# State mixing of a two-layer hybrid block: chunks of 128 tokens, two heads at a time, against chunks of 64 tokens, all heads at once

## What is computed

```python
def step(S, inp):
    r_t, w_t, k_t, v_t, kk_t, a_t = inp
    sa = jnp.einsum('bhvk,bhk->bhv', S, -kk_t)
    S = (S * w_t[:, :, None, :] + sa[..., None] * (kk_t * a_t)[:, :, None, :]
         + v_t[..., None] * k_t[:, :, None, :])
    return S, jnp.einsum('bhvk,bhk->bhv', S, r_t)
S0 = jnp.zeros((bsz, A_HEADS, A_HEAD_DIM, A_HEAD_DIM), f32)   # 8 heads of 64 x 64
_, o = lax.scan(step, S0, xs)
```

## Time and profile before

| | |
|---|---|
| median of 3 executions | 1030.74 us (1028.5 to 1035.65) |
| span of the profiled execution | 1026.6 us |
| what lies around the span, median less span | 4.1 us |
| PE busy | 1008.1 us |
| DVE busy | 816.6 us |
| ACT busy | 616.9 us |
| DMA, mean | 160 GB/s |

### The profile page before, as it was taken

How to read it: one execution, slowest core, us unless ns; L and a number is a source line. 1 busy time by engine, 2 the same in 40 slices (tenths; PEclk the granted TensorE clock), 3 DMA queues, 4 the chain that set the end, 5 groups by cost and what they waited for, 6 DMA issues and landing times.

```text
span 1026.6 us, 22212 instructions
## 1 busy us (share of the span) xinstructions
PE 1008.1 (98%) x8278; PEld 932.0 (91%) x8278; DVE 816.6 (80%) x1365; ACT 616.9 (60%) x967; POOL 11.9 (1%) x30
## 2 busy tenths in 40 slices
PE   8999999999999999999999999999999999999997
PEld 7998988899999999999999989789999999998886
DVE  6799763897797898878778996649977878888785
ACT  7964333656556665666689533246656565667665
POOL 0000000100000000000000000010000000000000
PEclk9999999999999999999999999999999999999999
DMA  8452342335545565555544534224445545565554
GB/s 301 148 182 103 104 146 81 114 111 178 162 154 179 180 209 183 189 185 184 191 142 145 185 99 144 88 74 142 139 153 167 182 164 185 172 219 185 192 192 152
DMA packets 46392, 164.42 MB, mean 160 GB/s; under 512 B 5888, under 2 KB 6064, under 8 KB 46304
## 3 DMA queue, kind: packets, MB, share of 16 engines
q1 hardware_dynamic: 44640, 160.19, 46.8%
q0 software_dynamic: 800, 1.33, 0.6%
q10 hardware_dynamic: 864, 1.63, 0.5%
HBM read 161.56 MB, written 1.05 MB: 158 GB/s over the span
## 4 chain that ended last, share of the span: by engine, by line
PE 86%; DVE 9%; ACT 2%; issue 2%; DMA 1%; SPq 0%; DVEq 0%; ACTq 0%
PE psum L471 85%; DVE sb_lo L1317 2%; ACT sb_rw L927 1%; DVE sb_inv L1566 1%; DVE sb_inv L1525 1%; DMA sb_x<-x_t 1%; DVE sb_inv L1528 1%; PE psum L789 1%; ACT sb_hh L927 0%; DVE sb_rw L1609 0%; DVE sb_yf L1590 0%; DVE sb_qb L1375 0%; ACT sb_hi L927 0%; DVE sb_rw L1496 0%; DVE sb_inv L1502 0%
## 5 line engine op out<-in xcount | busy, mean ns | idle before, releaser
L927 ACT ACTIVATE sb_hi<-sb_raw 128x1024 fp32r<-128x1024 f32 (+1 forms) x298 | 310.4, 1052 | 170.7 <-PE psum L471 161.2
L1317 DVE TENSOR_TENSOR sb_lo<-sb_raw,sb_hi 128x1024 fp32r<-128x1024 f32 x296 | 358.0, 1219 | 53.2 <-ACT sb_hi L927 52.9
L471 PE MATMUL psum<-sb_hh,sb_hi 128*128 128x256 f32 x1184 | 344.2, 291 | 3.2 <-DVE sb_hl L1324 2.1
L471 PE MATMUL psum<-sb_hl,sb_hi 128*128 128x256 f32 x1184 | 335.3, 283 | 0.0
L471 PE MATMUL psum<-sb_hh,sb_lo 128*128 128x256 f32 x1184 | 335.1, 283 | 0.0
L471 PE MATMUL psum<-sb_o,sb_hi 128*128 128x256 f32 (+1 forms) x1376 | 276.0, 314 | 1.3 <-DVE sb_o L1338 1.3
L471 PEld LDWEIGHTS psum<-sb_hh,sb_hi 128*128 128x128 f32 x1184 | 227.0, 192 | 17.9 <-issue 10.9
L471 PEld LDWEIGHTS psum<-sb_o,sb_hi 128*128 128x128 f32 x1376 | 224.1, 191 | 14.6 <-DVE sb_o L1338 1.7
L471 PEld LDWEIGHTS psum<-sb_hl,sb_hi 128*128 128x128 f32 x1184 | 227.3, 192 | 0.8 <-issue 0.5
L471 PEld LDWEIGHTS psum<-sb_hh,sb_lo 128*128 128x128 f32 x1184 | 227.2, 192 | 0.0
L471 PE MATMUL psum<-sb_o,sb_lo 128*128 128x256 f32 x880 | 193.9, 283 | 0.0
(11 more groups left out here) (187 smaller groups left out, 1027.7 us busy)
## 6 DMA issues: line engine op xcount, KB each, us to landing
sb_raw<-w_stream SPq DMA_DIRECT2D x299, 512.0 KB, 3.3
sb_pm<-mix_par ACTq DMA_DIRECT2D x2, 512.5 KB, 3.4
y_t<-sb_rw SPq DMA_DIRECT2D x4, 256.0 KB, 2.1
sb_cf<-const_f SPq DMA_DIRECT2D x1, 550.0 KB, 9.3
sb_pm<-mix_par SPq DMA_DIRECT2D x1, 512.5 KB, 10.9
sb_raw<-w_stream SPq DMA_DIRECT2D x2, 256.0 KB, 4.4
sb_x<-x_t ACTq DMA_DIRECT2D x2, 256.0 KB, 4.4
sb_x<-x_t SPq DMA_DIRECT2D x1, 512.0 KB, 6.7
```

Source lines behind the costliest of these rows:

```text
L471: return pe.matmul(out, lhsT, rhs, start=start, stop=stop, skip_group_check=True)
L927: return act.activation(out, in_, func, scale=scale, bias=bias, **kw)
L1317: tt(lo[:, s, :], raw[:, s, :], hi[:, s, :].bitcast(F32), ALU.subtract).then_inc(lo_done, 1)
```

## The change

The chunk becomes 64 tokens: there are four of them (`q`, in natural order; two halves `b` of each old chunk `ch`), and the inverse needs the levels 16 and 32 alone. All four tiles of heads are worked at once: `X`, `Y`, `M1`, `ABT`, `KBT` and `yf` hold four tiles, so `mat` runs four times in place of eight, `m1` and `dxy` four times each in place of twelve, but over twice the heads. The recurrence is `u`, `s`, `as` for each chunk: `u q` applies the inverse (8 matmuls), `s q` adds the output and makes the new state (24), `as q` brings the state to the next chunk's right side and output (16). `kv` and `ov` (32 matmuls each) do what doesn't depend on the state. All are 64x64 by 64. The odd tiles lie with their halves of partitions swapped (`nat`), so that two tiles fill four quarters. The copies after `natv` and `natk` become three each (`natural`: one of 128x256, two of 64x256), `natk` runs twice, and `(natv)` and `(natk, 0)` stand with no slab between them on PE. From slab 20 to slab 40 the slabs are spread: one after each small step or pair of steps, on all three engines. The last slab before the stage and the first behind it (D40) are the same.

```diff
+LEVELS = (16, 32)
-    ("prepb",), ("rk",), ("bon",), ("blk",), ("sel",), ("natv",), ("sol", 0), ("natk",), ("sol", 1), ("mat", 0,
...
+    ("prepb",), ("rk",), ("bon",), ("blk",), ("sel",), ("natv",), ("sol", 0), ("natk", 0), ("sol", 1),
+    ("mat", 0, "ab"), ("mat", 1, "ab"), ("sol", 2), ("mat", 0, "akb"), ("sol", 3), ("mat", 1, "akb"), ("sol", 4),
+    ("back",), ("place",), ("natk", 1), ("m1", 0, 16), ("m1", 1, 16), ("dxy", 0, 16), ("dxy", 1, 16), ("m1", 0, 32),
+    ("m1", 1, 32), ("dxy", 0, 32), ("dxy", 1, 32), ("kv",), ("u", 0), ("ov",), ("s", 0), ("as", 1), ("u", 1),
+    ("s", 1), ("as", 2), ("u", 2), ("s", 2), ("as", 3), ("u", 3), ("o",),
 STEPS = placed(
+    "+ D0-2 +3 D3-4 + D5 + D6 + D7-9 +4 D10-14 + D15-18 + D19 +5 D20 +3 D21 +2 D22 +2 D23 +2 D24 +2 D25 +2 D26 +2 "
...
-        yf = sb("yf", [P, 2, 4, C])
+        yf = sb("yf", [P, BT, 4, HD])
+        BKn2 = unit(2).rearrange("p (a c) -> p a c", a=2)
+        KV = unit(6).rearrange("p (q h c n) -> p q h c n", q=2, h=2, c=BT)
+        NU = unit(5).rearrange("p (q c h n) -> p q c h n", q=4, c=2, h=2)
+        def nat(c, b):
+            return BLK[b ^ (c & 1)]
 # PE, mat
+                    for cc in (2 * c, 2 * c + 1):
+                        for ch in range(2):
+                            split = what == "ab" and cc & 1
+                            for part in ((0,), (1,)) if split else ((0, 1),):
+                                for b in range(2):
+                                    to = BLK[b] if what == "ab" and part[0] == 0 and cc & 1 else nat(cc, b)
+                                    for hp in range(2):
+                                        last = mm(bank[b0 + hp][to, at],
+                                                  src[rows, cc, ch * C + HD * b:ch * C + HD * (b + 1)], rhs, first, True)
 # PE, dxy, level 16
+                        pe.wait_ge(dve_["mat"], n_of("mat", l, 4))
+                        pe.wait_ge(act_["natk"], n_of("natk", l, 2))
 # PE, the recurrence
+                elif kind == "u":
+                        pe.wait_ge(dve_["as"], n_of("as", l, c))
+                    for k in range(2):
+                        for hp in range(2):
+                            for odd in range(2):
+                                cc = 2 * k + odd
+                                last = mm(bank[6][nat(cc, b), col:col + HD], yf[BLK[b], cc, 2 * hp + ch, :],
+                                          KV[BLK[b], ch, hp, cc, :], k == hp == 0, True)
+                elif kind in ("s", "o"):
+                    pe.wait_ge(act_["u"], n_of("u", l, q + 1))
+                elif kind == "as":
+                    pe.wait_ge(dve_["s"], n_of("s", l, c))
+                    for cc in range(BT):
+                        for hp in range(2):
+                            mm(bank[5 + 2 * (b ^ (cc & 1))][BLK[hp], cols], s0[BLK[hp], cc, :],
+                               AR[BLK[hp], cc, ch, 1, BLK[b]], False, False)
+                    for cc in range(BT):
+                        for hp in range(2):
+                            last = mm(bank[3 + hp][BLK[b], cc * HD:(cc + 1) * HD], AR[BLK[hp], cc, ch, 0, BLK[b]],
+                                      s0[BLK[hp], cc, :], cc == 0, True)
 # ACT
+            def natural(to, src):
+                do(to[:, :, 0, :], src[:, :, 0, :], ACT.Copy)
+                for b, o in zip(BLK, OTHER):
+                    ins = do(to[o, :, 1, :], src[b, :, 1, :], ACT.Copy)
-                    do(Vn[:, 0, :], bank[3][:, :], ACT.Copy)
-                    do(Vn[:, 1, :], bank[7][:, :], ACT.Copy).then_inc(act_["natv"], 1)
+                    natural(Vn[:, 0, :], bank[3])
+                    natural(Vn[:, 1, :], bank[7]).then_inc(act_["natv"], 1)
 # ACT, natk
+                    if c:
+                        act.wait_ge(act_["place"], n_of("place", l, 1))
+                        act.wait_ge(dve_mid["place"], n_of("place", l, 1))
 # DVE, the recurrence
+                elif kind == "as":
+                    tt(to, to, banks(3)[BLK[b], :, 0:BT * HD], ALU.add).then_inc(dve_["as"], 1)
+                elif kind == "s":
+                    if c == 0:
+                        dve.tensor_copy(to, new).then_inc(dve_["s"], 1)
```

More of the change, by code:

```diff
@@ L154 @@
     TIMES[_s[0]] = ORD[_s] + 1
-X_STEP = {s: i for i, s in enumerate(s for s in STEPS if s[0] == "dxy" and s[2] < 64)}
+X_STEP = {s: i for i, s in enumerate(s for s in STEPS if s[0] == "dxy" and s[2] < LEVELS[-1])}
 X_STEPS = len(X_STEP)
@@ L165 @@
 BASE = 16
[L166 to L169, removed]
+CB = {"maskS": (0, 128), "mask64": (128, 128), "skip": (256, 384), "eye64": (640, 64)}
+CB.update({f"level{z}": (704 + 64 * i, 64) for i, z in enumerate(LEVELS)})
+NCB = 704 + 64 * len(LEVELS)
 PM, _o = {}, 0
@@ L182 @@
 ACT_OWN = {"turn": 0, "layer": 16}
-DVE_OWN = {"turn": 8, "layer": 125}
+DVE_OWN = {"turn": 8, "layer": 124}
 class Own:
@@ L362, in hybrid_blocks @@
                if k not in ("D", "E", "xs", "gsig", "prepa", "prepb", "rk", "kkn", "kkq", "lora", "gn3", "gn4", "rope",
-                            "sel", "sol", "back", "place")}
+                            "sel", "sol", "back", "place", "ov")}
         act_ = {k: sem("act_" + k) for k in TIMES
-                if k not in ("D", "E", "xs", "norm", "prepa", "prepb", "bon", "mat", "m1", "dxy", "rhs0", "s1", "rhs1",
+                if k not in ("D", "E", "xs", "norm", "prepa", "prepb", "bon", "mat", "m1", "dxy", "s", "as", "ov",
                              "rope", "gsig", "blk", "sol")}
         dve_ = {k: sem("dve_" + k) for k in TIMES
-                if k not in ("D", "E", "xs", "norm", "lora", "up", "kkq", "kk", "natv", "natk", "u0", "u1", "o", "gsig",
+                if k not in ("D", "E", "xs", "norm", "lora", "up", "kkq", "kk", "natv", "natk", "u", "ov", "o", "gsig",
                              "ct", "cav", "blk")}
@@ L648, in step @@
                 elif kind == "natk":
[L650 to L655, removed]
+                    if c == 0:
+                        pe.wait_ge(dve_["prepb"], n_of("prepb", l, 1))
+                        pe.wait_ge(dve_["rk"], n_of("rk", l, 1))
+                        pe.wait_ge(act_["natv"], n_of("natv", l, 1))
+                    else:
+                        pe.wait_ge(dve_["mat"], n_of("mat", l, 3))
@@ L663, in step @@
                         pe.wait_ge(act_["natk"], n_of("natk", l, 1))
                         pe.wait_ge(dve_["sel"], n_of("sel", l, 1))
[L665 to L672, removed]
+                    b0, src = 3 + 2 * (i % 2), A_ if what == "ab" else K
@@ L676, in step @@
                     if s[2] == LEVELS[0]:
-                        pe.wait_ge(dve_["mat"], n_of("mat", l, ORD[("mat", c | 1, "akb")] + 1))
-                        pe.wait_ge(dve_["place"], n_of("place", l, c // 2 + 1))
-                    else:
[L680 to L688, removed]
+                        pe.wait_ge(dve_["mat"], n_of("mat", l, 3 + c))
+                        pe.wait_ge(dve_["place"], n_of("place", l, 1))
+                    else:
+                        pe.wait_ge(x_done, l * X_STEPS + X_STEP[("dxy", c, LEVELS[0])] + 1)
+                    for cc in (2 * c, 2 * c + 1):
+                        for i in range(4):
+                            cols = slice(((cc & 1) * 4 + i) * HD, ((cc & 1) * 4 + i + 1) * HD)
+                            for b, o in zip(BLK, OTHER):
+                                last = mm(bank[4 + 2 * c][o, cols], ABT[b, cc, i, 0:HD], X[b, cc, i, :],
+                                          cc == 2 * c and i == 0, True)
                     last.then_inc(pe_["m1"], 1)
@@ L693, in step @@
                     if s[2] == LEVELS[0]:
[L694 to L703, removed]
-                        for b, o in zip(BLK, OTHER):
-                            if s[2] < LEVELS[-2] or b == BLK[0]:
-                                mm(bank[4 + 2 * j][b, cols], Y[o, j, i, :], M1[o, j, i, :], i == 0, True)
-                            last = mm(bank[5 + 2 * j][o, cols], M1[o, j, i, :], Y[o, j, i, :], i == 0, True)
@@ new lines, in step @@
+                        pe.wait_ge(act_["place"], n_of("place", l, 1))
+                        pe.wait_ge(dve_mid["place"], n_of("place", l, 1))
+                        pe.wait_ge(dve_["mat"], n_of("mat", l, 4))
+                        pe.wait_ge(act_["natk"], n_of("natk", l, 2))
+                    else:
+                        pe.wait_ge(dve_["dxy"], n_of("dxy", l, ORD[("dxy", c, LEVELS[0])] + 1))
+                    for cc in (2 * c, 2 * c + 1):
+                        for i in range(4):
+                            cols, first = slice(((cc & 1) * 4 + i) * HD, ((cc & 1) * 4 + i + 1) * HD), cc == 2 * c and i == 0
+                            for b, o in zip(BLK, OTHER):
+                                if s[2] < LEVELS[-1]:
+                                    mm(bank[4 + 2 * c][b, cols], Y[o, cc, i, :], M1[o, cc, i, :], first, True)
```

(12 more changed lines are left out.)

276 lines of the change are left out of this document (153 added, 123 removed), and 33 rows, old and new, of tables (ACT_STEPS, DVE_STEPS, STEPS, WORK).

## The result

| | before | changed |
|---|---|---|
| median | 1030.37 us (4 runs, 1028.5 to 1035.65) | 1015.36 us (4 runs, 1014.71 to 1016.18) |
| ratio | | 0.9857 [0.9827, 0.9886] |
| span of the profiled execution | 1026.6 us | 1014.1 us |

What follows compares the result with a forecast made beforehand. PE bounds the kernel (busy 98%). Per layer, slabs 59.0, groups 29.3 and waits 2.1 make 90.4 for 102.2; less 1.5 for clock, gain 10.3, twice 20.6: 1030.7 to 1010.1 us, range 1002 to 1021.

Steps and rivals of the forecast that it cites:

- the price of small matmuls: PE's small groups: 0.106 us per 64x64 by 64 unit in the longest quarter's queue, plus 0.23 a group.
- the rivals of quarters that don't overlap: New small groups on PE take twice their units, 11.5 us a layer: 1033 us, no change; chance 0.05.
- dearer forms: `u`, `s`, `as` cost up to twice their units, 6.1 us a layer: 1022; within the third case's 0.20.
- the one that stays low: Clock low through the recurrence, D30 to D40, 28 us more a layer: 1063 us, slower; chance 0.03.
- Gotcha 1: PSUM Pressure: Row halves writing one bank (`m1`, last `dxy`, `as`) would queue: 6.4 us a layer, 1023; within the third case's 0.20.
- The rival of ten waits: Ten recurrence groups each wait 0.5 us for ACT or DVE, 5 us a layer: 1020; within the third case's 0.20.
- the first hole: Between `natv` and `natk`, PE waits about 2.7 us for ACT's six copies of `natv`.
- the first fall: From `blk` to slab 20 the thin stretch drops PE's clock once, losing 1.5 us a layer; bounds 0 and 3.0.
- The rival with a held clock: Clock does not fall in the stage, all else as forecast, without 3.0: 1007 us; chance 0.30.
- the wait before `m1`: PE, through slab 25 at 103.8, waits 0.9 us for DVE's chain after `back`, ending at 104.6.
- the way from `m1` to `dxy`: ACT copies `natk 1`, then slab 27's halves, then `m1`'s first product at 110.9; PE waits 1.2 us before `dxy`.
- the prediction's third case: Waits in the recurrence, or forms or banks somewhat dearer: 1015 to 1023 us; chance 0.20.

Runs made afterwards that it cites:

- run 4: Changed kernel with ACT signalling after the first three of `natv`'s six copies, on which alone `natk 0` depends: 1010.57 us.
- run 9: Changed kernel with the spreading undone in the recurrence: slabs 30 to 39 behind `o` on all three engines; 1036.19 us.
- run 1: Changed kernel with 20 matmuls of 128x256, whose results nobody reads, added on PE ahead of `natk 0`'s wait: 1012.61 us.
- Run 3: Changed kernel with the high half of slab 26 moved ahead of the last solving step in ACT's list: 1011.28 us.
- Run 5: Changed kernel with the high halves of slabs 26 and 27 both moved ahead of the last solving step on ACT: 1010.17 us.
- runs 4 and 6: The second of these is the changed kernel with run 4's early signal and Run 5's ACT list together: 1005.28 us.
- the repeat: The changed kernel run once more, unedited, as the mark for the follow-up runs: 1014.93 us.

## Why the prediction was right, and where it was off

**Right: the price of small matmuls.** From the start of a group to the next slab, forecast and measured in layer 0: `mat ab` 1.93 and 1.97 (86.98 to 88.95); `mat akb` 1.08 and 1.04; last `dxy` with `kv` 2.78 and 2.95; `u 0` with `ov` 1.50 and 1.55; `s` 0.87 and 0.85 (136.59 to 137.44); `as` 1.08 and 1.08; `u` 0.65 and 0.61; `o` 0.44 and 0.39 (171.34 to 171.73). With this the rivals of quarters that don't overlap and of dearer forms are out, and the clock of 1.00 from `dxy` to slab 40 rules out the one that stays low. One of the prediction's own signs of being wrong did come, a group of 32 matmuls over 2 us: `m1` took 2.50 and 2.73 (108.86 to 111.36, 607.50 to 610.23). It was the second clock fall and not the quarters, as `m1` at full clock shows next. The rule of the Trainium skill, TensorEngine Tiling (Array Packing), Gotcha 1: PSUM Pressure, would have made each `as` 1.5 and `m1` 3.6; `as` took 1.08, and `m1` at full clock 2.01 (run 4, 106.39 to 108.40), so here too the trace does not agree.

**Right: the recurrence without waits.** PE's timeline shows none there, and run 9 shows what the cover is worth: nine waits of 0.5 to 1.5 us a layer without it. The rival of ten waits was its case without the cover.

**Right: the first hole and the first fall.** Hole 2.7 forecast, 2.58 measured, with ACT's six copies behind it. Clock 1.5 a layer forecast, 1.5 measured by run 1 against three of four traced layers; the fourth lost 2.7, within the bounds of 0 and 3.0. The rival with a held clock fell.

**Wrong: the wait before `m1`.** The step read: `back` starts at 100.55, "then `back` itself 0.74, a split of 1.13, and four products", and PE "waits 0.9 for it". DVE's chain was as long as said: `sol 1` to `back` 15.65 us (87.43 to 103.08), forecast 15.5. But the split was priced as DVE's work alone. Its high half has a place of its own in ACT's list, behind ACT's part of `back`, and that kept DVE waiting 1.75 us. The wait was 2.44. Run 3 takes exactly the 1.75 off.

**Too small: the way from `m1` to `dxy`.** Forecast 6.3 (104.6 to 110.9), measured 6.9. The step let ACT copy `natk 1` as soon as DVE had placed; it left out ACT's own part of `place`, two ACTIVATEs, 1.41 us (109.72 on), beside DVE's 0.87. The chain in the changed kernel, ACT (first fence) and DVE (second):

```profile
109.72 1.41 ACT L978 ACTIVATE sb_inv<-sb_rw,sb_cf 128x256 f32<-128x256 f32 x2 [4.29 <-DVE sb_rw L1625]
111.17 1.54 ACT L978 ACTIVATE sb_rw<-psum 64x256 f32<-64x256 f32 x4
112.73 1.06 ACT L978 ACTIVATE sb_hi<-sb_raw 128x1024 fp32r<-128x1024 f32 x1
```

```profile
113.89 1.22 DVE L1395 TENSOR_TENSOR sb_lo<-sb_raw,sb_hi 128x1024 fp32r<-128x1024 f32 x1 [3.29 <-ACT sb_hi L978]
115.03 1.28 DVE L1652 TENSOR_TENSOR sb_rw<-psum,sb_cb 128x512 f32<-128x512 f32 x2
```

ACT places, copies `natk 1` and only then makes the high half of slab 27; DVE's low half waits for it, and the first product of `m1` stands behind. Run 5 moves the high half ahead, and the distance is 5.07. The wait of 1.2 was therefore 1.8 at full clock. The second clock fall, which was not forecast, falls inside it and cost nothing.

**The sum.** Per layer the forecast was 91.9 for the stage (90.4 and 1.5 for the clock); measured 95.4 in layer 1 and 96.6 in layer 0. `m1` started at 32.59 where 30.7 was forecast (104.6 less 75.4, and 1.5): 1.9, of which 1.75 is ACT's queue. Then 0.6 up to `dxy`. The rest, 55.96 from `dxy` to slab 40 against 54.9 (90.4 less 110.9 - 75.42), is 1.0: of the thirteen slabs there nine last 3.07 us (133.52 to 136.59) or nearly so, not 3.0, the four of values 2.95, not 2.83, and the groups together 0.2 more; 0.3 had been allowed for. Together 3.5; layer 0 adds 1.2 for the longer fall. Both layers make 8.2, and the span missed its forecast of 1006.0 by 8.1. The median missed by 5.3 only (1015.4 for 1010.1), and the difference is luck. The 4.1 us taken for what lies around the span was median less span. In every later execution of the kernel before, the time is 1.8 to 1.9 above its own span, so the profiled one must have taken about 1028.5, like the fastest of the four; the rest of the 4.1 was its distance from the median. The profiled execution of the changed kernel took 1016.18, 2.1 above its span but 0.8 above its median, so median less span is 1.3 there. By its number the result even falls into the prediction's third case (1015 to 1023), but not one of the causes given for that case is in the trace; the time went ahead of `m1` and `dxy`.

## What to carry to other kernels

When PE's small work shrinks, follow the chain that it then waits on through every queue which that chain crosses: a step shared by two engines has a place in both lists, and the copy on the idle engine can be the one that decides. Before pricing a clock fall or a wait, ask whether a fixed chain of another engine runs beside it, for then the two hide each other and must be taken away together. With a recurrence of short dependent steps, independent work between them can be worth more than fewer or smaller matmuls.

## What was unexpected of the hardware

- The clock does not follow the length of a hole alone. The hole of 2.58 us before `natk 0` was followed by a fall in both profiles of the changed kernel and by none in layer 0 of run 9, where `m1` starts at 31.10 as in run 1; the hole of 2.43 before `m1` was followed by a fall in one layer of run 4 and not in the other. After 1.4 us (runs 4 and 6, four layers) there was none.
- The same hole led to half clock for 6.7 us in layer 0 of one profile, a loss of 2.7, and to a loss of 1.5 in the other layer and in both of the repeat. Why stays open.
